# A one-core decoder layer: samples' cached values summed by rows on VectorE, with six reorderings

## What is computed

```python
n = rms_norm(x, g_mix); proj = n @ w_in                 # q | k | v | h | B | C
q, k = rms_norm(q, q_norm), rms_norm(k, k_norm)         # per head of 64
# prompt: causal attention over dilated windows (1, 4, 16), 16 heads
# sample: the new key and value and 256 cached ones
s = einsum('bshd,bsjhd->bshj', q, kg) * scale + bias
o = einsum('bshj,bsjhd->bshd', exp(s - m), vg) / den
conv = B * short_conv(C * h)
h += concat(rms_norm(attn), rms_norm(conv)) @ w_out
h += (silu(n @ w_gate) * (n @ w_up)) @ w_down
h += sigmoid(rms_norm(h) @ w_ple_gate) * (p @ w_ple_proj)
```

## Time and profile before

| | us |
|---|---|
| median of 3 runs | 2514.38 (2513.5 to 2515.45) |
| the profiled execution | 2514.97 |
| its span, first to last instruction | 2513.4 |
| TensorE busy | 2471.6 (98%) |
| VectorE, ScalarE, GpSimd busy | 1754.7, 943.5, 253.0 |
| one pass of the loop over pairs | 82.7, VectorE busy 63.4 of it |
| mean granted TensorE clock | 0.995 of 2.4 GHz |

### The profile page before, as it was taken

How to read it: one execution, slowest core, us unless ns; L and a number is a source line. 1 busy time by engine, 2 the same in 40 slices (tenths; PEclk the granted TensorE clock), 3 DMA queues, 4 the chain that set the end, 5 groups by cost and what they waited for, 6 DMA issues and landing times.

```text
span 2513.4 us, 51724 instructions
## 1 busy us (share of the span) xinstructions
PE 2471.6 (98%) x20366; PEld 2455.4 (98%) x20366; DVE 1754.7 (70%) x2203; ACT 943.5 (38%) x1225; POOL 253.0 (10%) x281
## 2 busy tenths in 40 slices
PE   7999999999989999999999999999999999999998
PEld 7999999999989999999999999999999999999998
DVE  5777787778776899888888888888433323456332
ACT  5343334333433454444444444444322211233331
POOL 1120111011100001000000000000000000143000
PEclk9999999999989999999999999999999999999999
DMA  6352333333333424343333334343665443233331
GB/s 209 119 159 95 125 109 126 114 111 111 121 126 101 156 85 152 126 143 128 123 134 117 134 119 148 125 144 118 214 211 170 160 145 116 80 92 104 108 113 67
DMA packets 99741, 324.00 MB, mean 129 GB/s; under 512 B 18258, under 2 KB 18514, under 8 KB 99168
## 3 DMA queue, kind: packets, MB, share of 16 engines
q1 hardware_dynamic: 72144, 250.25, 30.4%
q0 software_dynamic: 26672, 70.69, 8.2%
q10 hardware_dynamic: 864, 2.24, 0.2%
HBM read 286.80 MB, written 40.65 MB: 130 GB/s over the span
## 4 chain that ended last, share of the span: by engine, by line
PE 94%; DVE 2%; DMA 2%; issue 1%; ACT 1%; SPq 0%; POOL 0%; DVEq 0%; ACTq 0%
PE acc L566 18%; PE acc L570 18%; PE acc L568 18%; PE acc L769 12%; PE acc L770 12%; PE acc L768 11%; DMA wraw<-in_w_down 1%; PE aux L577 1%; PE aux L615 1%; DMA hid<-in_x_tiles 1%; PE aux L659 1%; PE aux L605 0%; PE aux L604 0%; DVE wlo L1266 0%; PE aux L628 0%
## 5 line engine op out<-in xcount | busy, mean ns | idle before, releaser
L1266 DVE TENSOR_TENSOR wlo<-wraw,whi 128x1024 fp32r<-128x1024 f32 (+1 forms) x276 | 333.6, 1209 | 371.8 <-ACT whi L907 371.0
L907 ACT ACTIVATE whi<-wraw 128x1024 fp32r<-128x1024 f32 (+1 forms) x276 | 285.4, 1034 | 680.0 <-PE acc L570 610.9
L768 PE MATMUL acc<-xb_hi,whi 128*128 128x260 f32 x1228 | 347.6, 283 | 4.4 <-DVE xb_lo_t L1664 4.4
L769 PE MATMUL acc<-xa_lo,whi 128*128 128x260 f32 x1228 | 348.3, 284 | 0.0
L770 PE MATMUL acc<-xa_hi,wlo 128*128 128x260 f32 x1228 | 348.3, 284 | 0.0
L770 PE MATMUL acc<-xb_hi,wlo 128*128 128x260 f32 x1228 | 347.3, 283 | 0.0
L768 PE MATMUL acc<-xa_hi,whi 128*128 128x260 f32 x1228 | 346.7, 282 | 0.0
L566 PE MATMUL acc<-slots_a,whi 128*128 128x260 f32 x1536 | 312.7, 285 | 0.0
L570 PE MATMUL acc<-slots_a,wlo 128*128 128x260 f32 x1536 | 308.9, 282 | 0.0
L568 PE MATMUL acc<-slots_a,whi 128*128 128x260 f32 x1536 | 308.8, 283 | 0.0
L566 PE MATMUL acc<-slots_b,whi 128*128 128x260 f32 x1392 | 280.9, 283 | 3.6 <-ACT hid L1205 3.3
(11 more groups left out here) (298 smaller groups left out, 5059.4 us busy)
## 6 DMA issues: line engine op xcount, KB each, us to landing
wraw<-in_w_in SPq DMA_DIRECT2D x96, 512.0 KB, 3.5
blocks<-in_w_gate SPq DMA_DIRECT2D x88, 512.0 KB, 6.0
blocks<-in_w_up SPq DMA_DIRECT2D x88, 512.0 KB, 6.0
wraw<-in_w_down SPq DMA_DIRECT2D x48, 448.0 KB, 3.4
wraw<-in_w_out SPq DMA_DIRECT2D x32, 512.0 KB, 3.5
wraw<-in_w_ple_gate SPq DMA_DIRECT2D x32, 512.0 KB, 3.5
slots_b<-f_dram SPq DMA_DIRECT2D x28, 520.0 KB, 4.5
f_dram<-sig_t POOLq DMA_DIRECT2D x22, 520.0 KB, 3.2
```

Of the source, the lines that this page charges most:

```text
L768: mm(to, w_h, hi, start=p == 0, stop=False)
L769: mm(to, w_h, lo, start=False, stop=False)
L907: on(whi[:, u % HILO, 0:width], wraw[:, u % RAW, 0:width], ACT.Copy).then_inc(s_whi, 1)
L1266: V.tensor_tensor(wlo[:, u % HILO, 0:width], wraw[:, u % RAW, 0:width], whi[:, u % HILO, 0:width].bitcast(F32), ALU.subtract).then_inc(s_w ...
```

## The change

The samples' cached values come from the host with channels on the partitions and positions along the row. VectorE puts the new value into column 256 of each sample's row (g = 8). The 16 rows of probabilities are stored to DRAM and loaded again spread over 64 partitions for each of the two heads (`p_rows`); VectorE multiplies the 8 x 257 values by them and sums along the row (g = 9). TensorE has no part in it any more. The mask tile skew now lies in p_rows, kv in the tile of values, and `o_low` in gate_t (v_t in the last attention). So the keys and the mask of the next pair are loaded after the row sum.

The reorderings: in the first pass VectorE copies v and k out ahead of the squares' additions; in the conv stage the last query's norm moves behind the second residual tile, and q's halves behind the attention step; the last values are loaded at tile 8 and not 6; two sums of combined blocks go ahead of the fifth weight block at the start of gate and up; the first down chunk and the per-layer projection use four accumulators and not two. The waits on s_row, s_out are renumbered throughout (not shown below).

```diff
...
+    p_dram = nc.dram_tensor("p_dram", (KA, DEC, 2, ROW_W), F32, kind="Internal").ap()
...
+    skew = p_rows.rearrange("p b i -> p (b i)")[:, 0:2 * SEQ].rearrange("p (e s) -> p e s", e=2)
     prob = sb("prob", [P, 2, SEQ], scope=mix)
     pthi = sb("pthi", [P, QB, 2, P], F32R, mix)
     ptlo = sb("ptlo", [P, QB, 2, P], F32R, mix)
     stats = sb("stats", [P, 3], scope=mix)
-    kv = sb("kv", [P, DEC * KCACHE, P], scope=mix)
+    cached = sb("cached", [P, DEC, ROW_W], scope=mix)
+    kv = cached.rearrange("p b i -> p (b i)")[:, 0:DEC * PAST].rearrange("p (n f) -> p n f", f=P)
     qkv_s = sb("qkv_s", [P, 3, DEC], scope=mix)
     kq_s = sb("kq_s", [P, DEC], scope=mix)
     kq_pair = sb("kq_pair", [P, DEC, 2], scope=mix)
     key_sc = sb("key_sc", [P, KCACHE, 2 * DEC], scope=mix)
     row_bias = sb("row_bias", [2 * DEC, ROW_W], scope=mix)
     row_stats = sb("row_stats", [2 * DEC, 3], scope=mix)
-    new_diag = sb("new_diag", [2 * DEC, 2 * DEC], scope=mix)
-    p_cols = sb("p_cols", [P, 3, 2 * DEC], scope=mix)
-    out_s = sb("out_s", [P, DEC, 2], scope=mix)
     mix.close()
 
 
...
     t_odd = tmp[:, 0:2, :].rearrange("p a t -> p (a t)").rearrange("p (n h) -> p n h", h=HALF)
+    def o_low(final):
+        return (v_t if final else gate_t)[:, 0:SEQ]
...
                     nc.tensor.transpose(aux[0:2 * DEC, BANK_D, t * P:(t + 1) * P], key_sc[:, t, :], ident[:, :])
                 mm(aux[0:2 * DEC, BANK_D, PAST:PAST + 1], kq_pair[:, :, :], ones[:, 0:1],
                    start=True, stop=True).then_inc(s_str, 1)
-            if g == 7:
-                pe.wait_ge(s_row, 5 * a + 5)
-                mm(aux[:, BANK_D, KCACHE * 2 * DEC:(KCACHE + 1) * 2 * DEC], ones[0:2 * DEC, :], new_diag[:, :],
-                   start=True, stop=True)
-                for t in range(KCACHE):
-                    done = nc.tensor.transpose(aux[:, BANK_D, t * 2 * DEC:(t + 1) * 2 * DEC],
-                                               row[:, t * P:(t + 1) * P], ident[0:2 * DEC, 0:2 * DEC])
-                done.then_inc(s_str, 1)
-            if g == 9:
-                if not final:
-                    pe.wait_ge(s_root, 2 * a + 3)
-                pe.wait_ge(s_wv, 3 * a + 3)
-                for b in range(DEC):
...
                     pe.wait_ge(s_biased, 8 * a + 8)
-                    pe.wait_ge(s_pc, a + 1)
+                    pe.wait_ge(s_row, 4 * a + 1)
...
                     pe.wait_ge(s_xwide, 1)
                 pe.wait_ge(s_sq, 2 * j + 1)
...
-                pe.wait_ge(s_out, 4 * a + 2)
 
         def pair(at, j, a):
...
-        pe.wait_ge(s_out, 4 * (KA - 2) + 2)
         column_sums(acc_conv).then_inc(s_nsum, 1)
         unit(at, 1, mixed, (KC - 1,), 1, False, True, n0=KC - 1)
...
-                pe.wait_ge(s_read, i * 4 + (T_D + b - 1))
-                unit(Span(U_D, 4, i), b, *down_units(0, 0), b % 2, True, True)
+                pe.wait_ge(s_read, i * 4 + (T_D + b - 3))
+                unit(Span(U_D, 4, i), b, *down_units(0, 0), b % 2, True, True, to=first_down(b))
         for c in range(1, CHUNKS):
             with pe.Fori(0, KT // 2) as i:
...
-                pe.wait_ge(s_read, T_PLE + m - 1)
+                if m >= 2:
+                    pe.wait_ge(s_read, T_PLE + m - 3)
                 for kt in range(KP):
                     at_n = slice((kt * PT + n) * P, (kt * PT + n + 1) * P)
                     for h in range(2):
-                        done = products(acc[:, m % 2, h, 0:HALF], whi[:, i % HILO, at_n], wlo[:, i % HILO, at_n],
+                        done = products(first_down(m % 4)[:, h, :], whi[:, i % HILO, at_n], wlo[:, i % HILO, at_n],
                                         p_slot(kt)[:, 0, h * HALF:(h + 1) * HALF],
                                         p_slot(kt)[:, 1, h * HALF:(h + 1) * HALF],
                                         kt == 0, kt == KP - 1)
                 done.then_inc(s_unit if n == PT - 1 else s_pm, 1)
...
         spread_sum(ones, acc_h).then_inc(s_nsum, 1)
...
+                    if final:
+                        act.wait_ge(d_v, 16 * KA)
+                    else:
+                        act.wait_ge(s_conv, a + 1)
                 act.wait_ge(s_pv, 4 * a + 2 * (e + 1))
-                on(o_low[e * HD:(e + 1) * HD, :], aux[(1 - e) * HD:(2 - e) * HD, BANK_O, :], ACT.Copy).then_inc(s_olow, 1)
+                on(o_low(final)[e * HD:(e + 1) * HD, :], aux[(1 - e) * HD:(2 - e) * HD, BANK_O, :], ACT.Copy).then_inc(s_olow, 1)
             if g <= 7:
                 w = (g % QB + 1) * P
...
+                    act.wait_ge(d_p, 16 * a + 16)
                 root_of(qk_rstd, HD).then_inc(s_root, 1)
...
+            if 3 <= i <= PAIR_UNITS + 2:
+                attention(KA - 1, i - 3, final=True)
+            if i < KA - 1:
+                operand_hi(KC + i, hid[:, i, :], ROWS["attn"] + i).then_inc(s_xhi, 1)
             if i == 1:
                 q_hi(KA - 1)
-            if 3 <= i <= PAIR_UNITS + 2:
-                attention(KA - 1, i - 3)
-            if i < KA - 1:
-                operand_hi(KC + i, hid[:, i, :], ROWS["attn"] + i).then_inc(s_xhi, 1)
             if i == 13:
                 act.wait_ge(s_o, 2 * KA)
...
         sums_hi(EARLY)
         sums_hi(EARLY + 1)
+        sums_hi(EARLY + 2)
         block_hi(Span(U_G), 0, 0, HILO)
-        sums_hi(EARLY + 2)
...
-        def first_copy(i, b, source=None):
+        def first_copy(i, b):
             m = i * 4 + b
             act.wait_ge(s_unit, m + (U_D + 1))
-            on(halves(hid[:, m, :]), acc_of(b % 2) if source is None else source, ACT.Copy).then_inc(s_read, 1)
...
+                dve.wait_ge(s_row, 4 * a + 3)
                 V.tensor_scalar(row[:, :], row[:, :], row_stats[:, 2:3], None, ALU.mult).then_inc(s_row, 1)
-                dve.wait_ge(s_row, 5 * a + 4)
-                V.tensor_scalar(new_diag[:, :], ident[0:2 * DEC, 0:2 * DEC], row[:, PAST:PAST + 1], None,
-                                ALU.mult).then_inc(s_row, 1)
-            if g == 7:
-                dve.wait_ge(s_str, 2 * a + 2)
-                V.tensor_copy(p_cols.rearrange("p t c -> p (t c)"), aux[:, BANK_D, 0:3 * 2 * DEC]).then_inc(s_pc, 1)
-                dve.wait_ge(s_pc, a + 1)
+            if g == 8:
                 dve.wait_ge(l_vc, 16 * a + 16)
-                for t in range(KCACHE):
-                    V.tensor_tensor(cached(t), cached(t), p_cols[:, t, :].rearrange("p (b e) -> p b e", b=DEC)
-                                    .unsqueeze(3).broadcast_to([P, DEC, 2, HD]), ALU.mult).then_inc(s_wv, 1)
-                dve.wait_ge(s_wv, 3 * a + 2)
-                V.tensor_tensor(cached(0), cached(0), cached(1), ALU.add).then_inc(s_wv, 1)
-            if g == 8:
-                V.tensor_tensor(out_s[:, :, :], qkv_s[:, 2, :].unsqueeze(2).broadcast_to([P, DEC, 2]),
-                                p_cols[:, KCACHE, :].rearrange("p (b e) -> p b e", b=DEC), ALU.mult).then_inc(s_out, 1)
-            if g == 10:
-                dve.wait_ge(s_out, 4 * a + 1)
-                dve.wait_ge(s_spv, a + 1)
-                if not final:
-                    dve.wait_ge(s_root, 2 * a + 4)
-                V.tensor_tensor(out_s[:, :, :], out_s[:, :, :],
-                                aux[:, BANK_D, 0:DEC].unsqueeze(2).broadcast_to([P, DEC, 2]), ALU.add).then_inc(s_out, 1)
-                dve.wait_ge(s_out, 4 * a + 2)
-                for e in range(2):
-                    V.tensor_copy(hid[e * HD:(e + 1) * HD, a, SEQ:T], out_s[e * HD:(e + 1) * HD, :, e]).then_inc(s_out, 1)
-
-        def cached(t):
-            return kv.rearrange("p (b t) (e d) -> p t b e d", t=KCACHE, e=2)[:, t, :, :, :]
+                V.tensor_copy(cached[:, :, PAST], qkv_s[:, 2, :]).then_inc(s_out, 1)
+            if g == 9:
+                dve.wait_ge(l_p_rows, 32 * a + 32)
+                dve.wait_ge(s_out, 3 * a + 1)
+                V.tensor_tensor(cached[:, :, :], cached[:, :, :], p_rows[:, :, :], ALU.mult).then_inc(s_out, 1)
+                dve.wait_ge(s_out, 3 * a + 2)
+                V.tensor_reduce(hid[:, a, SEQ:T], cached[:, :, :], X, ALU.add).then_inc(s_out, 1)
 
         def keys_times_q(e):
             part = kv.rearrange("p (b t) f -> p b t f", t=KCACHE)[:, 4 * e:4 * e + 4, :, :]
...
-            if a is None and g < 4:
-                for t in X_SQUARES[g]:
-                    if t > 0:
-                        dve.wait_ge(s_xsq, t + 1)
-                        if t > 1:
-                            dve.wait_ge(s_xadd, t - 1)
-                        V.tensor_tensor(x_sum, x_sum, tmp[:, t % 2, :], ALU.add).then_inc(s_xadd, 1)
...
+            if a is None and g < 4:
+                for t in X_SQUARES[g]:
+                    if t > 0:
+                        dve.wait_ge(s_xsq, t + 1)
+                        if t > 1:
+                            dve.wait_ge(s_xadd, t - 1)
+                        V.tensor_tensor(x_sum, x_sum, tmp[:, t % 2, :], ALU.add).then_inc(s_xadd, 1)
             if g == 5:
...
+            if i == 1:
```

(43 more changed lines are left out.)

39 lines of the change are left out of this document (19 added, 20 removed).

## The result

The changed kernel takes 2523.15 us (median of 6 runs, 2522.22 to 2526.27) where the kernel before takes 2514.12 (6 runs): a ratio of 1.0037, 95% interval 1.0025 to 1.0050, so 9 us slower. The forecast was 2512.5 and no change. The result lies in the range of the prediction, but on the slower side of the forecast. It is the number of the third rival, though that rival's cause carries only a part of it.

What follows compares the result with a forecast made beforehand. TensorE runs back to back and VectorE's stretch from the key's reciprocal to q's low half has no slack. Savings of -38.4 us against +36.4 give -2.0 on 2514.97, so 2513.0, a median of about 2512.5; range 2486 to 2526.

Steps and rivals of the forecast that it cites:

- third rival: Loop: GpSimd's squares meet the query's scaling or taps, six waits 1.3 longer, clock falls each time: 2523 us; chance 0.22.
- first copies: First pass: v's copy ahead of four additions frees TensorE 3 us sooner, column sums wait 0.8: -3.8 us.
- last query's norm: Conv stage: norm behind the second residual tile removes a wait of 4.4, some 3.6 returns a unit later: -1.3 us.
- sums ahead of block 4: Start of gate and up: of a 4.4 us wait some 2.1 stay, fourth block's split holds TensorE 1: -2.7 us.
- four accumulators, projection: First down chunk and projection: waits of 3.3 and 1.0 us shrink or go, -2.8 and -1.0: -3.8 us.
- six waits at the score: Loop: TensorE's first score waits for VectorE's longer chain, 3.4 us in each of six passes: +20.4 us.
- their clock falls: Loop: TensorE's clock drops to 1.2 GHz behind four of the six new waits, 1.6 us each: +6.4 us.
- second mask: Second pair: the mask's load, now issued after the row sum, lands late and holds up VectorE and TensorE: +5.5 us once.
- conv product: Last pair of the loop: conv product moves about +1.7 while TensorE comes 2.4 earlier: +4.1 us.
- hidden way through DRAM in step 9: Each pair: probabilities' store and spread load land by 411, used after the addition at 415.55: cost nothing.
- The first rival: Loop: no new wait, as VectorE's freed time carries over or the sum is hidden: 2483 us; chance 0.17.
- The fourth: Loop: probabilities land after VectorE asks, each further microsecond from 5 us late costs 7: over 2530 us; chance 0.06.

Runs made afterwards that it cites:

- two_cols: The changed kernel with multiplication and row sum of the cached values covering only 2 of each sample's 257 columns: 2486.46 us.
- q_first: The changed kernel with q's low half ahead of the five conv taps on VectorE, not behind them: 2524.35 us.
- squares_late: The changed kernel with GpSimd's squares of the attention output moved behind the wait for the conv product: 2526.10 us.
- mask_first: The changed kernel with the second pair's mask loaded ahead of the last store of masks in GpSimd's queue, first pass only: 2517.91 us.
- act_sum: The changed kernel with the row sum on ScalarE in the loop's passes, as eight copies with an accumulated sum: 2518.71 us.
- combo: The changed kernel with multiplication in step 8, row sum on ScalarE, mask's load ahead of the keys and last mask store behind both: 2503.68 us.

## Why the prediction was wrong, point by point

| term, us | predicted | in the traces |
|---|---|---|
| TensorE's work removed | -19.0 | -19 (a pass of 80.3 in two_cols) |
| first copies | -3.8 | -0.4 (-0.8 to -2.2 in nine other runs) |
| last query's norm | -1.3 | -4.8, then +1.7 |
| values later | -7.8 | -7.7 (10.1 less 2.4) |
| sums ahead of block 4 | -2.7 | -0.5 |
| four accumulators, projection | -3.8 | -5.7 |
| six waits at the score | +20.4 | +23.9 |
| their clock falls | +6.4 | +11 |
| second mask | +5.5 | +4.8 |
| conv product | +4.1 | +5.8 |
| sum | -2.0 | +9 |

**The mechanism was right, its size was off.** VectorE's freed time could not be carried forward, the sum landed in a stretch without slack, and six waits of over 3 us followed, as predicted. What failed are sizes in the sum. Five terms together came out 15.4 us worse than they were put: the clock by 4.6, the six waits by 3.5, the first copies by 3.4, the sums ahead of block 4 by 2.2, the conv product by 1.7. The last query's norm, the accumulators and the mask gave 4.4 of it back, and so a forecast of no change became 9 us.

**The clock is the largest of them.** The prediction had a fall in four of six waits, 6.4 us; it fell at six, for 11. The argument for four was that the new wait of 3.4 us "lies by the first", the wait of 3.45 of before behind which it fell. The waits were longer (3.73 at least). The length of a wait alone doesn't tell either: in the changed kernel the clock falls behind a wait of 1.5 (the window from 51.42 on) and holds behind the 1.6 before 727.51. In q_first, where the same score waits 1.6 too (724.12), it falls (0.50 from 727.40 to 730.70).

**The waits.** 3.5 us of the miss is here. squares_late divides it: 3.67 us of each wait is there without the squares, 0.27 over the predicted 3.4 and 1.6 us in six. The two instructions are 4.8 long with their gap, and the prediction's 4.5 for them was already less than its own rows add up to (2.36 + 2.34 = 4.7). The other 1.9 is contention: 1.0 and 0.5 in the first two passes from a slowed copy and scaling, 0.4 in the other four. The prediction put the squares on the reciprocal. The first of their two instructions was there, and the second ran over its end.

**First copies.** The prediction let the column sums wait 0.8 and the clock hold. They waited 1.5, and behind them TensorE ran 7.5 us at 0.54: 3.4 us, nearly all that the edit had saved in this execution.

**The conv product** was 2.8 late, and the fall of the clock behind it (7.00 us at 0.53) was in no term. The last query's norm brought 3.1 and not 1.3: the old wait of 4.4 had carried a clock fall of its own (0.50 from 696.24 to 700.74 in the kernel before), which the prediction left out. At the start of gate and up the sums brought 0.5 and not 2.7: TensorE still waits 2.0 and 1.1 there, and the clock falls in both kernels (for 3.4 us from 902.2 and from 915.4 on). The prediction's own parts, 4.4 less 2.1 less 1, make 1.3 unless that fall goes too. That the accumulators brought 5.7 and not 3.8 was not followed further.

**Right:** the work removed, the mask (4.8 against 5.5, its cause shown by mask_first), the values' load, the hidden way through DRAM in step 9, and the stages behind, which only shifted. The first rival (no new wait) falls with the waits. The fourth (probabilities late) falls with two_cols for step 9; they become late in the first pass as soon as they are wanted in step 8. The third rival gave the right time by luck, with a sum that was wrong in its parts: of its 8 us of contention 2 were there, its six falls of the clock cost 11 and not 9.6, and the rest of the way came from the chain's own length, the first copies, the sums and the conv product.

**What the prediction lacked altogether:** it measured slack at q's low half, as if the score were the only thing that waits for that stretch. q_first shows the next one, the first prob, with 2.5 us of the same lateness. For the time of this change both readings give the same sum; for a repair only the second one works.

## What to carry to other kernels

Look for stretches in which one engine works without a gap, from an input it waits for to a result another engine waits for. Price a change by the work that enters or leaves such a stretch. Try a repair by taking work out of it (into a gap inside it, or onto an engine that stands), and not by exchanging its instructions. Before blaming the instruction that releases a wait, look for what is waited for next from the same engine. When a piece leaves such a stretch, or leaves another queue, ask what the instructions and transfers of the other engines now lie beside: the same 2.4 us of squares cost a reciprocal nothing and two copies of eight columns up to 1.8 us, and with the squares moved away a weight's load took 8.7 us and not 4.7.

## What the runs showed of the hardware that was not expected

- A VectorE copy of 128 x 8 in SBUF, 0.17 us, takes 1.16 beside GpSimd's squares (changed kernel, 176.80), 0.96 beside GpSimd's issue of a transfer alone (act_sum, 173.03), and 1.71 or 1.95 beside both (act_sum, combo); a reciprocal of 520 columns keeps its 3.40 beside them.
- The granted clock fell to 1.2 GHz behind a wait of 1.5 us (at 51.42) and not behind one of 1.6 (at 727.51) in the same execution. In combo it held behind two waits of 2.2 and 2.1 (at 434.24 and 517.05) and fell behind two others of 2.1 (350.10, 599.86).
- ScalarE's copies of 257 columns with an accumulated sum start every 0.40 us, eight in 3.3 us: only 1 us dearer than VectorE's one sum over 2056 (2.29), on an engine that stood.
